# Value panels of the gated feed-forward by seven block products, their weight sums between output tiles

## What is computed

```python
def swiglu(h, w_in, w_out):
    gu = h @ w_in
    gate, up = jnp.split(gu, 2, axis=-1)
    return (jax.nn.silu(gate) * up) @ w_out
...
        x = x + g2 * swiglu(h, ffn_w_in[i], ffn_w_out[i])
```

## Time and profile before

| | |
|---|---|
| median of 3 runs | 2545.11 us (2544.84 to 2545.34) |
| the profiled execution | 2544.84 us, span 2543.1 us |
| granted TensorE clock | 0.999 of full |
| TensorE busy | 2514.6 us, 99% |
| VectorE, ScalarE, GpSimd busy | 1321.6, 764.7, 1422.2 us |
| the two gated stages, by their stretch | 1618 to 1935 us and 2188 to 2500 us |

### The profile page before, as it was taken

How to read it: one execution, slowest core, us unless ns; L and a number is a source line. 1 busy time by engine, 2 the same in 40 slices (tenths; PEclk the granted TensorE clock), 3 DMA queues, 4 the chain that set the end, 5 groups by cost and what they waited for, 6 DMA issues and landing times. The chain is left out here.

```text
span 2543.1 us, 37266 instructions
## 1 busy us (share of the span) xinstructions
PE 2514.6 (99%) x15183; PEld 2062.2 (81%) x15183; DVE 1321.6 (52%) x2134; ACT 764.7 (30%) x1483; POOL 1422.2 (56%) x796
## 2 busy tenths in 40 slices
PE   8999999999999999999999999999999999999999
PEld 6787778888887877788888767788888888788888
DVE  4445565666534346656665344655554135755554
ACT  5245451111123454511011443322222333422223
POOL 5543246666565423356655833677776522677776
PEclk9999999999999999999999999999999999999999
DMA  8321034555333211445562211223233211232232
GB/s 268 83 61 51 22 112 149 191 188 185 115 101 83 62 49 34 133 138 181 195 199 100 70 51 36 89 94 99 99 99 126 83 51 35 83 98 99 98 99 71
DMA packets 220459, 265.50 MB, mean 104 GB/s; under 512 B 19236, under 2 KB 192892, under 8 KB 220188
## 3 DMA queue, kind: packets, MB, share of 16 engines
q1 hardware_dynamic: 217628, 256.72, 31.4%
q10 hardware_dynamic: 2688, 6.76, 0.8%
HBM read 258.74 MB, written 4.72 MB: 104 GB/s over the span
## 5 line engine op out<-in xcount | busy, mean ns | idle before, releaser
L923 POOL TENSOR_SCALAR WH<-RAW 128x2048 fp32r<-128x2048 f32 x112 | 215.4, 1924 | 713.3 <-issue 608.7
L925 POOL TENSOR_TENSOR WL<-RAW,WH 128x2048 fp32r<-128x2048 f32 x112 | 519.0, 4634 | 9.3
L1115 PE MATMUL PS<-Hh,WL 128*128 128x512 f32 x864 | 337.3, 390 | 0.7 <-POOL WL L955 0.7
L1118 PE MATMUL PS<-Hl,WH 128*128 128x512 f32 x864 | 336.4, 389 | 0.0
L1119 PE MATMUL PS<-Hh,WH 128*128 128x512 f32 x864 | 336.1, 389 | 0.0
L3040 DVE SCALAR_TENSOR_TENSOR X<-PS,X 128x512 f32<-128x512 f32 x304 | 207.0, 688 | 185.5 <-PE PS L1868 123.3
L955 POOL TENSOR_TENSOR WL<-RAW,WH 128x512 fp32r<-128x512 f32 x192 | 277.7, 1474 | 4.0
L2775 ACT ACTIVATE PS<-SQ 128x512 f32<-128x512 f32 x64 | 38.5, 602 | 557.1 <-DVE SQ L3381 557.1
L1864 PE MATMUL PS<-U,WL 128*128 128x512 f32 x512 | 200.1, 391 | 0.0
L1867 PE MATMUL PS<-U,WH 128*128 128x512 f32 x512 | 199.2, 389 | 0.0
L1868 PE MATMUL PS<-U,WH 128*128 128x512 f32 x512 | 199.2, 389 | 0.0
(11 more groups left out here) (636 smaller groups left out, 5878.6 us busy)
## 6 DMA issues: line engine op xcount, KB each, us to landing
RAW<-in_w_ff SPq DMA_DIRECT2D x64, 1024.0 KB, 5.3
PROJ<-in_ada_w SPq DMA_DIRECT2D x48, 1024.0 KB, 7.9
RAW<-in_ffn_w_in SPq DMA_DIRECT2D x44, 1024.0 KB, 5.1
RAW<-in_ffn_w_out SPq DMA_DIRECT2D x22, 1024.0 KB, 4.9
RAW<-in_w_in SPq DMA_DIRECT2D x20, 1024.0 KB, 5.3
RAW<-in_w_out SPq DMA_DIRECT2D x8, 1024.0 KB, 5.1
RAW<-in_a_w_in SPq DMA_DIRECT2D x6, 1024.0 KB, 5.0
RAW<-in_b_w_in SPq DMA_DIRECT2D x12, 512.0 KB, 5.1
```

The lines of the kernel that those rows point to most:

```text
L923: pool.tensor_scalar(WH[b][:, :], RAW[b][:, :], 1.0, 1.0, ALU.mult, ALU.mult).then_inc(s.split_hi, 1)
L925: pool.tensor_tensor(WL[b][:, :], RAW[b][:, :], WH[b][:, :].bitcast(F32), ALU.subtract).then_inc(s.split_done, 1)
L1115: ins = mm(bank, WL[b][:, col:col + P], Hh[:, k, :], start=k == 0, stop=False)
L1118: mm(bank, WH[b][:, col:col + P], Hl[:, k, :], start=False, stop=False)
```

## The change

`FAST` becomes (0, 1): from chunk 2 on, the value panels too are computed by seven block products, nine per stage. Their weight sums, copies, combinations and splits come with it. The order of the work changes in three places. On VectorE all four gate weight sums stand ahead of the value's first combination; the value weight sums for chunk c+2 stand between the adds of D(c)'s first tiles, and these ahead of the gated products of chunk c+1; adds 5 and 6 stand behind the gated products, adds 7 and 8 behind the low halves. On ScalarE the high parts of the gate sums stand between the two copies of the value's `copies`, and those of the value sums ahead of the high parts of U.

```diff
--- before.py
+++ after.py
@@ -52,7 +52,7 @@
 DIL = 4
 D_FF2 = 2816
 FF2_CHUNKS = D_FF2 // 256
-FAST = (0,)
+FAST = (0, 1)
 FAST_FROM = 2
 FAST_PANELS = len(FAST) * (FF2_CHUNKS - FAST_FROM)
 PARTS = 16 * LAYERS + 20
@@ -2793,11 +2793,13 @@
                         act.wait_ge(s.f_evac, c * 8 + (f0 + BANKS - 8))
                     f(PS[:, 3 * z + 1, 0:256], PS[:, 3 * z, 0:256], ACT.Copy).then_inc(fa.copied, 1)
 
-                def copies(z, c):
+                def copies(z, c, ahead=False):
 
                     n = number(z, c)
                     act.wait_ge(fa.products, fa.products_0 + (n * 5 + 2))
                     f(p5_copy(z), PS[:, 3 * z + 2, 0:256], ACT.Copy).then_inc(fa.copied, 1)
+                    if ahead:
+                        sums_high(0, c + 1)
                     act.wait_ge(fa.products, fa.products_0 + (n * 5 + 4))
                     f(p167_copy(z), PS[:, 3 * z + 1, 0:256], ACT.Copy).then_inc(fa.copied, 1)
 
@@ -2837,10 +2839,12 @@
                             act.wait_ge(fa.sums, fa.sums_0 + ((FAST_PANELS * 4 + 9) * w + x + 2))
                             f(h_sums_hi(x), h_sums(x), ACT.Copy).then_inc(fa.sums_hi, 1)
                     if value_fast:
-                        copies(1, c)
+                        copies(1, c, ahead)
+                    elif ahead:
+                        sums_high(0, c + 1)
                     if ahead:
-                        sums_high(0, c + 1)
                         panel_high(0, c + 1, b0)
+                        sums_high(1, c + 1)
                     for j in range(2):
                         if value_fast:
                             act.wait_ge(s.u_in, c * 2 + (u0 + 2))
@@ -2851,8 +2855,6 @@
                         else:
                             act.wait_ge(s.u_in, c * 2 + (u0 + j + 1))
                             f(U[:, e, j, 0, :], PS[:, 3 + j, :], ACT.Copy).then_inc(s.uhi, 1)
-                    if ahead:
-                        sums_high(1, c + 1)
 
                 chunk(0, 0, False, False, normed=True)
                 chunk(1, 1, False, True)
@@ -3493,20 +3495,20 @@
                         v.wait_ge(fa.sums_hi, fa.sums_hi_0 + ((FAST_PANELS + 4) * w + x + 1))
                         v.tensor_tensor(h_sums_lo(x), h_sums(x), h_sums_hi(x).bitcast(F32), ALU.subtract).then_inc(fa.sums, 1)
 
-                def hidden(c, e, fast, ahead=None):
+                def hidden(c, e, fast, ahead=None, between=None):
 
                     gate_fast, value_fast = (fast and z in FAST for z in range(2))
                     if gate_fast:
                         combine_first(0, c)
                         combine(0, c)
                     if ahead:
-                        weight_sums(0, c + 1, *ahead[0], range(2))
+                        weight_sums(0, c + 1, *ahead[0], range(4))
                     if value_fast:
                         combine_first(1, c)
-                    if ahead:
-                        weight_sums(0, c + 1, *ahead[0], range(2, 4))
+                        combine(1, c)
+                    if between:
+                        between(0)
                     if value_fast:
-                        combine(1, c)
                         v.wait_ge(fa.combined, fa.combined_0 + (number(1, c) * 4 + 4))
                     halves = range(2) if value_fast else range(1)
                     for j in range(2):
@@ -3518,6 +3520,8 @@
                             ins = v.tensor_tensor(x, y, x, ALU.mult)
                         if len(halves) == 1 or j:
                             ins.then_inc(s.u_in, len(halves))
+                    if between:
+                        between(1)
                     for j in range(2):
                         v.wait_ge(s.uhi, c * 2 + (u0 + (2 if len(halves) == 2 else j + 1)))
                         for h in halves:
@@ -3532,12 +3536,18 @@
 
                 def chunk(c, e, fast, ahead):
 
-                    hidden(c + 1, e, fast, ahead)
-                    for i in range(4):
-                        add(c, range(i, i + 1))
-                        if ahead:
-                            weight_sums(1, c + 2, *ahead[1], range(i, i + 1))
-                    add(c, range(4, KT))
+                    def between(x):
+
+                        if x:
+                            add(c, range(4, 6))
+                            return
+                        for i in range(4):
+                            if ahead:
+                                weight_sums(1, c + 2, *ahead[1], ((0, 1), (2,), (3,), ())[i])
+                            add(c, range(i, i + 1))
+
+                    hidden(c + 1, e, fast, ahead, between)
+                    add(c, range(6, KT))
 
                 def panel_loaded(c, z, c2=None):
```

## The result

The changed kernel takes 2605.79 us (median; 2605.14 to 2606.43) against 2544.98: a ratio of 1.0239, 95% interval 1.0226 to 1.0251, so 60.8 us slower. The forecast was 2601, range 2562 to 2633.

A forecast was written before the change was run, and what follows sets the result against it. TensorE bounds the kernel now; after the change a ring over several engines would, at 35.1 us a period against 31.85. That gives 28.2 us a stage, 56 us for two, so 2601 us, range 2562 to 2633.

The forecast's parts named there:

- What bounds it, and the products: Gated stages: TensorE's own stream bounds them now; 18 value panels go from 10.91 to 10.07 us, 0.84 us each.
- The ring: Value panel's begin to second load issue 9.3, first value sum 5.13, VectorE's block 13.0, copy 0.47, gate blocks 7.2: 35.1 us.
- VectorE's block: VectorE, first value sum to add 8: eight adds 5.44, eight halves 2.72, four sums 4.8, together 13.0 us.
- The sums beside GpSimd: VectorE weight sums: gate sums about 1.65 us each beside GpSimd; value sums one at 1.7, three at 1.0 to 1.1.
- Strict turns: Rival: VectorE sums and GpSimd pieces exclude each other, up to 1.95 us a sum; period 36.8, total 2633 us; chance 0.10.
- The wait of 2.8 us at the value's fifth block: TensorE waits there for VectorE's first combination, ready at 19.5 us from the gate's start but needed at 16.7.
- The 0.9 at the gate's third block and 0.3 at its start: TensorE waits each period: 0.9 us for ScalarE's copy into bank 1, 0.3 us for add 5.
- The clock: A lower TensorE clock from its new idle time, some 12% of a period, was left out at no cost.
- 28.2 us a stage: Added time per gated stage: eight longer periods 26.0 us, run-in 2.2, last chunk about 0; 56 us for two stages.
- TensorE staying the bound: Rival: VectorE's block takes at most 9 us, the ring closes in 31.0, 15 us come off: 2530 us; chance 0.09.
- Value sums free of GpSimd: Rival: GpSimd finishes the next gate split first, value sums cost 2.8 us; period 33.1, total 2563 us; chance 0.08.
- 14%: Chance of the two cases outside the range: TensorE the bound (2530 us, 0.09) and waits balancing the gain (2545 us, 0.05).

The follow-up runs named there:

- kernel a: Changed kernel with two of the four gate weight sums ahead of the value's first combination and two behind it; 2601.66 us.
- kernel h: Kernel a plus a VectorE reduction over 1536 elements between add 4 and the gated products; 2645.51 us.
- kernel k: Kernel a plus a VectorE reduction over 1536 elements between the gate's first combination and the rest of them; 2601.48 us.
- i: Changed kernel with the gated products directly behind the value's last combination, nothing else moved; 2634.73 us.
- kernel e: Kernel before the change with two VectorE reductions of 1536 elements in front of the gate's first combination; 2605.29 us.
- g: Changed kernel with the down panel's high part taken by ScalarE, not GpSimd, from chunk 2 on; 2598.09 us.

## Why the prediction was right, point by point

- *What bounds it, and the products.* Confirmed. The two panels by seven products take 20.16 us where nothing waits (the last pair of the first stage), against 10.07 + 10.91; the 0.82 us gained are what the earlier trace rows gave.
- *The ring.* Right link by link: 35.1 us forecast, 35.24 measured in kernel a, 35.25 in the changed kernel's last six periods. Its decisive term, VectorE's block at 13.0 us, is 13.0 to 13.1, the two bounds having been 11.0 and 15.0. In the changed kernel the value panels of the settled periods begin 35.20 to 35.27 us apart, however much its gate panels alternate. In the period of V's begin at 1785.98 it is 14.45 to the first value sum, 13.03 for the block, 0.45 to the gate's third block and 7.30 to the next V at 1821.21. Kernels h and k show that the block is a link and VectorE's load is not. The 0.34 us for a 256-wide half, which no row showed, is 0.33 (four in 1.32 from start to start).
- *The sums beside GpSimd.* Beside GpSimd's pieces 1.68 us from start to start on average for the four gate sums and 1.69 for the second value sum, and 1.05 for the two between adds, as taken. Strict turns, as the Trainium skill (SBUF — State Buffer, "Who interferes with whom") has them, would cost 1.95 us for each pair and by the prediction's walk make the period 36.8; the trace says otherwise, with four gate sums in 6.70 us and a period of 35.25, as it did before the change.
- *Where TensorE waits.* Partly right. The wait of 2.8 us at the value's fifth block is there in the six settled periods, at 2.6. The 0.9 at the gate's third block and 0.3 at its start are there as 0.6 and 0.6, but only in every third period. The 0.9 and 0.3 were expected in every period. What takes their place in the other two is the clock, next point.
- *The clock.* Wrong. I left it out, from a first slice of the page with TensorE busy for 8 tenths and a full clock. Behind the 2.6 us wait TensorE ran at the lower level for about 3.5 us in two of three settled periods, and for 5.7 us behind each of the first two waits of the stage, which were 4.0 us long. In the settled periods it cost next to nothing, because V's blocks 5 to 7 and D are not in the ring: a slow stretch there only uses up the waits at the gate's start and third block. That it fits is luck, and by very little. Behind a slow stretch no wait is left at the next gate panel, and TensorE's own path sets the time: 18.44 us from the gate's start at 1740.64 to V's fifth block at 1759.08 and 16.83 from there to the next gate panel at 1775.91, together 35.27, beside 35.24 for the ring. That is also why 34.4, 36.1 and 35.3 us alternate around 35.25 between gate panels, and why kernel a at full clock has the same period. The step that was wrong is the term put at nothing; it should have been priced: where the slow stretch falls on ring blocks, as in h and i, it lengthens the period.
- *The sum.* 28.2 us a stage were forecast. The medians give 30.4 on average, the profiled execution 32.7 in the first stage and 28.9 in the second. In the first stage: the run-in cost 1.4 us and not 2.2 (1665.17 against 1663.76); the first two periods 6.0 and 5.7 and not 3.25, by the longer waits and the clock behind them; the other six 3.4 each; and the last chunk kept its gain, 42.03 against 42.84 us from its gate panel to the stage's end, where I had it given back. So 2601 lies within 5 us of 2605.79 partly by luck: 0.8 too much in the run-in and 0.8 too much in the last chunk hide some of the 5.2 us that the first two periods took beyond the forecast. What led to waits of 4.0 us there, and not of 2.6, was not followed up.
- *The rivals.* TensorE staying the bound needed a block of 9 us and failed by 4. Value sums free of GpSimd did not come, for the reason given. Kernel a, at full clock and without the long waits, ends 4.1 us below the changed kernel, so the clock as a rival would have moved the sum by a few microseconds. One result does not show whether 14% was the right weight for faster or unchanged.

## What to carry to other kernels

When a step makes the full engine's work shorter but hangs more small steps of other engines on it, don't add up their loads; follow one buffer around (begin of a panel, split, load, sums, adds, bank free, next panel) and sum that ring with durations at their contended values. If it is longer than the full engine's period, removing the largest visible wait only moves it (kernel a), and the order of work on the in-order engines decides more than their load (42 us between two orders of the same instructions). The same reduction costs 44 us in the ring, the lower clock that it brings included, and nothing beside it.

## What the runs showed of the hardware

- A wait of TensorE of 2.3 to 2.6 us in the middle of a dense stream was followed by about 3.4 us at the 1.2 GHz level in some cases and not in others of the same length: 9 of 13 waits of 2.6 us in the changed kernel, 7 of 18 in kernel e. Behind every wait of 3.8 to 4.3 us it was lower, for 3.4 to 5.7 us (3 waits in the changed kernel, 16 in i, 3 in g). In kernel a, with several waits a period of at most 1.3 us and a single one of 2.5 us in the second stage, the clock stayed at 1.00 in both stages. What decides in the cases between was not settled.
- A VectorE sum of two SBUF operands, 128 by 512, takes 0.68 us alone and up to 1.78 beside GpSimd's pieces; those that stood between two PSUM adds took 1.02 to 1.05 from start to start, also with GpSimd at work. The reduction over 1536 elements of one SBUF operand took the same 1.74 us beside GpSimd's pieces (kernel k) as in the block (kernel h).
